# Projections of an attention block computed from high and low parts, and a small gate projection issued on four column strips

## The reference

```
h = modulate(rms_norm(x, norm_mix), shift, scale)          # latent and context tokens
qa, ka, va, qb, kb, vb = split(h @ e_w_in)                 # 512, 128, 128, 512, 512, 512 columns
qa, ka, qb, kb = rms_norm per head of 64; qa, ka get rope on the latent tokens
o_a = window_attention(qa, ka, va, ka_c, va_c, sink)       # 8 query heads, 2 key/value heads
o_b = neighbourhood_attention(qb, kb, vb, kb_c, vb_c, rpb) # 8 heads, a bias table per head
x = x + g1 * (concat(o_a, o_b) @ e_w_out)                  # then a squared-relu MLP
```

```
qkv, z, ba, sc_p, fn_u = split(h @ w_in)                   # ba: 16 columns
beta = sigmoid(ba[:8]);  g = -exp(a_log) * softplus(ba[8:] + dt_bias)
qkv = silu(conv(qkv)) ...                                  # chunked delta rule, gates, merge, SwiGLU
```

## Time and profile before

| | |
|---|---|
| median of 3 runs | 1873.57 us (1872.82 to 1874.22) |
| profiled execution | 1871.45 us, span 1869.6 us |
| busy in the span | PE 1780.8 us (95%), DVE 913.7 (49%), ACT 614.3 (33%), POOL 125.4 (7%) |
| weight loads (PEld) | 1337.9 us (72%) |
| data moved in the first of 40 slices | 388 GB/s, mean of the span 136 GB/s |

### The profile page before, as it was taken

One profiled execution on the slowest core, in us unless ns is written; L12 is line 12 of the kernel. 1 busy time (PEld: TensorE's weight loads), 2 busy tenths in 40 slices (PEclk: granted clock), 3 DMA queues, 4 the chain that ended last, 5 costly groups with the idle time before them and its releaser, 6 DMA issues.

```text
span 1869.6 us, 25422 instructions
## 1 busy us (share of the span) xinstructions
PE 1780.8 (95%) x10086; PEld 1337.9 (72%) x10086; DVE 913.7 (49%) x1704; ACT 614.3 (33%) x1155; POOL 125.4 (7%) x138
## 2 busy tenths in 40 slices
PE   6998899999999999898999999999899899999998
PEld 2443445478888887453679999648579799889997
DVE  2133764263434344345736665344468854445554
ACT  3112554142323232133635444302320044034433
POOL 1001000100000001033000000100115000000000
PEclk9999999999999999998999999899999999999999
DMA  9223774322222223244044443313230334344442
GB/s 388 78 90 146 292 278 186 117 104 95 90 91 90 90 91 144 103 156 162 19 156 157 181 181 137 135 61 125 85 135 1 111 132 165 135 150 168 165 155 85
DMA packets 20886, 253.89 MB, mean 136 GB/s; under 512 B 2208, under 2 KB 4512, under 8 KB 5024
## 3 DMA queue, kind: packets, MB, share of 16 engines
q1 hardware_dynamic: 17712, 242.44, 34.2%
q10 hardware_dynamic: 3056, 9.82, 1.4%
HBM read 251.20 MB, written 1.05 MB: 135 GB/s over the span
## 4 chain that ended last, share of the span: by engine, by line
PE 83%; DVE 8%; ACT 3%; DMA 3%; issue 2%; POOL 1%; DVEq 0%; POOLq 0%; SPq 0%; ACTq 0%
PE bank L498 26%; PE bank L524 13%; PE bank L525 13%; PE bank L526 13%; PE bank L924 4%; PE bank L586 3%; PE bank L661 3%; PE bank L684 2%; PE bank L669 2%; DVE w_lo L1582 1%; DMA weights<-in_ada 1%; ACT w_hi L1187 1%; POOL root L2034 1%; ACT slab L1127 1%; DMA weights<-in_even_in 1%
## 5 line engine op out<-in xcount | busy, mean ns | idle before, releaser
L498 PE MATMUL bank<-slab,weights 128*128 128x256 f32 (+2 forms) x1456 | 445.2, 464 | 3.0 <-DVEq L1691 1.2
L498 PEld LDWEIGHTS bank<-slab,weights 128*128 128x128 f32 (+1 forms) x1456 | 272.8, 189 | 169.7 <-issue 134.2
L1582 DVE TENSOR_TENSOR w_lo<-weights,w_hi 128x1024 fp32r<-128x1024 f32 (+1 forms) x220 | 264.4, 1211 | 93.6 <-ACT w_hi L1187 92.7
L1187 ACT ACTIVATE w_hi<-weights 128x1024 fp32r<-128x1024 f32 (+1 forms) x220 | 228.4, 1046 | 215.9 <-PE bank L526 209.6
L524 PE MATMUL bank<-h_hi,w_hi 128*128 128x256 f32 (+1 forms) x864 | 273.9, 317 | 8.5 <-DVE w_lo L1582 5.9
L525 PE MATMUL bank<-h_lo,w_hi 128*128 128x256 f32 (+1 forms) x864 | 273.4, 316 | 0.0
L526 PE MATMUL bank<-h_hi,w_lo 128*128 128x256 f32 (+1 forms) x864 | 272.0, 315 | 0.0
L524 PEld LDWEIGHTS bank<-h_hi,w_hi 128*128 128x128 f32 x864 | 162.9, 189 | 24.9 <-issue 11.4
L525 PE MATMUL bank<-mlp_hidden_lo,w_hi 128*128 128x512 f32 (+1 forms) x512 | 174.4, 341 | 0.0
L524 PE MATMUL bank<-mlp_hidden_hi,w_hi 128*128 128x512 f32 (+1 forms) x512 | 173.3, 338 | 0.6 <-DVE w_lo L1582 0.6
L526 PE MATMUL bank<-mlp_hidden_hi,w_lo 128*128 128x512 f32 (+1 forms) x512 | 172.7, 337 | 0.0
(11 more groups left out here) (209 smaller groups left out, 2305.2 us busy)
## 6 DMA issues: line engine op xcount, KB each, us to landing
weights<-in_ada SPq DMA_DIRECT2D x36, 2048.0 KB, 7.6
weights<-in_mlp_up SPq DMA_DIRECT2D x16, 2048.0 KB, 8.4
weights<-in_mlp_down SPq DMA_DIRECT2D x16, 2048.0 KB, 8.4
weights<-in_ffn_in SPq DMA_DIRECT2D x11, 2048.0 KB, 7.5
weights<-in_in SPq DMA_DIRECT2D x8, 2048.0 KB, 8.5
weights<-in_gate SPq DMA_DIRECT2D x6, 2048.0 KB, 7.6
weights<-in_ffn_out SPq DMA_DIRECT2D x8, 1408.0 KB, 6.0
weights<-in_even_in SPq DMA_DIRECT2D x4, 2048.0 KB, 13.2
```

The costliest lines, as they stand in the source:

```text
L498: last = mm(b[rows, 0:width], lhsT(k), rhs(k), start=k == 0, stop=k == kc - 1)
L1187: A(split_part(w_hi, q), raw_part(q), ACT.Copy).then_inc(sem("w_hi_ready"), 1)
L1582: V.tensor_tensor(split_part(w_lo, q), raw_part(q), split_part(w_hi, q).bitcast(F32), ALU.subtract)\
```

## The change

- The 14 items of the even projections (a fourteenth for the A heads' values) and the B heads' values use high and low parts. The A keys become item 0, the A queries 1 to 4, the B queries 5 to 8, the B keys 9 to 12. `split_norm` takes the place of the norm's scale and shift.
- The A heads' values are computed feature-major, copied to a buffer and turned by four transposes; the B heads' values use `w_hi` and `w_lo` as the moving operand, all four token groups open at once, over four parts of two chunks.
- Ropes, means and spreads are issued between the items (`even_steps`); the third group's spreads go two by two in side banks.
- The first weight block is loaded in four transfers with semaphores of their own for the first three.
- The `near` table lies where `h_lo` lay, is loaded when the last B value product has closed, and is prepared inside the attention, one head before each even unit from 16 to 30.
- The attentions wait for their values only ahead of the first product with them.
- beta and dt: strips of 32 output partitions as in `ada_block`, issued within key product 0 as the chunks of h come; ScalarE copies the strips; four small matmuls against `fold` add them and put the tokens first.
- `norm_root` is called ahead of `split_norm` instead of inside it.

The diff, cut to its core:

```diff
-SPLIT = {"mlp_up0", "mlp_down0", "mlp_up1", "mlp_down1", "ffn_in", "ffn_out", "gate"}
+SPLIT = {"even_in", "even_in_a", "mlp_up0", "mlp_down0", "mlp_up1", "mlp_down1", "ffn_in", "ffn_out", "gate"}
...
@@ TensorE, split_linear with lead
-                        for q, _ in opened_parts:
-                            pe.wait_ge(sem("w_hi_ready"), q + 1)
-                            pe.wait_ge(sem("w_lo_ready"), q + 1)
                         for k in range(kc - 2):
                             for mi, (q, b) in enumerate(opened_parts):
+                                if k == 0:
+                                    part_ready(q)
                                 triple(b, q, 0, k, mi)
...
@@ TensorE, even projections (the plain products are removed)
+            def even_steps(i):
+                if i == 4:
+                    pe.wait_ge(sem("c0_in"), 16)
+                if i % 4 == 0:
+                    means_of("even", i // 4 - 1)
+                if i in (5, 9):
+                    spread_of("even", i // 4 - 1)
+                if i in (7, 8, 9, 10):
+                    rope("even", i - 7)
+                if i == 11:
+                    rope("even", 4)
...
+            split_linear("even_in", range(3), h_high, h_low, TOK, lambda m: ("even", m),
+                         lambda k, m: pe.wait_ge(sem("mix0_h"), k + 1) if m == 0 else None, lead=True, after=even_steps,
+                         idle=(7, 0))
+            stream.append(["even_in_a", 0, None])
+            for at, t in enumerate((("even", 12), ("va", 0))):
+                q = next_part(at * PART * P, PART * P, t)
+                b = open_group(t)
...
+                if at == 0:
+                    means_of("even", 2)
+            means_of("even", 3)
+            stream.append(["even_in", 3, None])
+            vb = [open_group(("vb", t)) for t in range(4)]
+            for p in range(4):
+                q = next_part(p * PART * P, PART * P, ("vb", 3))
...
+                for t in range(4):
+                    rows = slice(t * P, (t + 1) * P)
+                    for k in range(2):
+                        j = 2 * p + k
+                        mm(vb[t][:, :], h_high(j)[:, rows], wh[:, k, :], start=j == 0, stop=False)
+                        mm(vb[t][:, :], h_high(j)[:, rows], wl[:, k, :], start=False, stop=False)
+                        ins = mm(vb[t][:, :], h_low(j)[:, rows], wh[:, k, :], start=False, stop=j == DC - 1)
...
+                if p == 0:
+                    drained(pe, ("va", 0))
+                    b = open_group(("va", 1), which=0)
+                    for t in range(4):
+                        rows = slice(t * P, (t + 1) * P)
+                        ins = nc.tensor.transpose(b[:, rows], prob[4][:, rows], ident)
+                    close(ins, ("va", 1))
+                if p < 2:
+                    spread_of("even", 2, 2 * p, 2, aside=True)
+                if p == 2:
+                    spread_of("even", 3, aside=True)
             pe.wait_ge(sem("even_roped"), 5)
-            for t in range(4):
-                drained(pe, ("va", t))
-                drained(pe, ("vb", t))
-            attention("even")
+            attention("even", [("va", 1)] + [("vb", t) for t in range(4)])
...
@@ TensorE, second stage
-            w = take_block("in2_ba", 0)
-            for t in range(4):
-                product(("ba", t), DC, lambda k: h[:, k, t * P:(t + 1) * P], lambda k: w[:, k, :], width=16,
-                        before=h_ready("mix2") if t == 0 else None, idle=12 if t == 0 else 0)
-            release_block(("ba", 3))
+            def gates_by_chunk(k):
+                pe.wait_ge(sem("mix2_h"), k + 1)
+                for j in range(k - 3, k + 1) if k % 4 == 3 else ():
+                    strip = slice(j % 4 * STRIP, (j % 4 + 1) * STRIP)
+                    ins = mm(b_ba[strip, :], w_ba[:, j, :], h[:, j, :], start=j < 4, stop=j >= 4)
...
+            def gates_tokens_first():
+                b = open_group(("ba", "tokens"))
+                drained(pe, ("ba", "strips"))
+                for t in range(4):
+                    ins = mm(b[:, t * 16:(t + 1) * 16], ba_row[:, t * P:(t + 1) * P], fold[:, 0:16], start=True, stop=True)
+                close(ins, ("ba", "tokens"))
...
+            for mi in range(4):
+                product(("k", mi), DC, lambda k: w[:, k, mi * P:(mi + 1) * P], lambda k: h[:, k, :],
+                        before=gates_by_chunk if mi == 0 else None, idle=12 if mi == 0 else 0)
+                if mi == 1:
+                    gates_tokens_first()
...
@@ SyncE, the first block of parts
+                if n == parts[0][0]:
+                    for q in range(PARTS):
+                        load(ring[n % RING][:, at:at + PART * P], dram[name][blk][:, at:at + PART * P], f"first_in{q}")
+                        at += PART * P
...
@@ ScalarE
-            norm_shift("mix0", TOK, 0, 0)
+            split_until(PARTS)
+            split_norm("mix0", TOK, 0, 0)
             for i in range(13):
-                if i == 3:
-                    load(near[:, :, :], dram["near"], "near_in")
                 if i == 6:
                     load(consts[:, N_C0:N_C0 + N_C1], dram["c1"], "c1_in")
+                split_until(PART_END[("even", i)] + PARTS)
                 item_raw("even", i)
...
+            for t in (0, 2):
                 copy_out(("vb", t), v0[:, t, 0:512])
+            filled(act, ("vb", 3))
+            load(near[:, :, :], dram["near"], "near_in")
             attention("even")
...
@@ VectorE, attention
+                    if name == "even" and 16 <= i < 32 and i % 2 == 0:
+                        dve.wait_ge(sem("near_in"), 16)
+                        hd = (i - 16) // 2
+                        link(V.scalar_tensor_tensor(out=near[:, hd, :], in0=near[:, hd, :], scalar=HD ** 0.5,
+                                                    in1=k0("near"), op0=ALU.mult, op1=ALU.add))
...
@@ VectorE, split_norm
                 for c in range(DC + 1):
+                    if name == "mix0" and c == 1:
+                        split_until(PARTS)
...
@@ VectorE, even projections
-            norm_scale("mix0", TOK, 0, 0)
+            split_norm("mix0", TOK, 0, 0)
...
+            for i in range(13):
+                split_until(PART_END[("even", i)] + PARTS)
+                if i >= 4 and i % 4 == 0:
+                    group_inverse("even", i // 4 - 1)
+                if i in (8, 9, 10, 11):
+                    rope("even", i - 8)
+                if i in (5, 9):
+                    group_scale("even", i // 4 - 1)
+                if i == 12:
+                    rope("even", 4)
+            split_until(PART_END[("va", 0)] + PARTS)
+            group_inverse("even", 3)
+            split_until(PART_END[("vb", 3)] + 1)
+            group_scale("even", 2)
+            group_scale("even", 3)
+            for t in (1, 3):
+                filled(dve, ("vb", t))
+                V.tensor_copy(v0[:, t, 0:512], bank(("vb", t))[:, :]).then_inc(free(("vb", t)), 1)
```

More of the change, by code:

```diff
@@ L435, in build @@
         ROPE = {
-            "even": ([qk[:, c, 0:LAT] for c in (0, 1, 2, 3, 12)], slice(0, P), k0("rot"), k0("cos"), k0("sin"), rtmp,
-                     [("even", c) for c in (0, 1, 2, 3, 12)]),
+            "even": ([qk[:, c, 0:LAT] for c in range(5)], slice(0, P), k0("rot"), k0("cos"), k0("sin"), rtmp,
+                     [("even", c) for c in range(5)]),
             "uq": ([q1[0:MLA_QK, i, :] for i in range(MLA_HEADS)], slice(0, MLA_QK), k1("rot96")[0:MLA_QK, :],
@@ L512, in linear, with part_ready, next_part, part_used @@
                     release_block(t)
-            def split_linear(name, blocks, hi, lo, width, tag, before=None, lead=False, idle=(0, 0)):
+            def part_ready(q):
+                pe.wait_ge(sem("w_hi_ready"), q + 1)
+                pe.wait_ge(sem("w_lo_ready"), q + 1)
+            def next_part(at, size, tag):
+                q = len(parts)
+                parts.append([len(stream) - 1, at, size, tag])
+                part_ready(q)
+                return q
+            def part_used(ins):
+                used[0] += 1
+                ins.then_inc(sem("part_used"), 1)
+                parts[-1][3] = used[0]
+            def split_linear(name, blocks, hi, lo, width, tag, before=None, lead=False, after=None, idle=(0, 0)):
                 rows, cols, _ = WEIGHTS[name]
@@ L648, in rope, with attention @@
                 close(mm(b[rows, 0:LAT], swap, acts[i], start=True, stop=True), t)
-            def attention(name, idle=0):
+            def attention(name, v_tags, idle=0):
                 a = ATT[name]
@@ L723, in _ @@
             ada_fold(0)
-            items = ITEMS["even"]
-            for blk in range(3):
-                w = take_block("even_in", blk)
-                for mi in range(4):
-                    i = blk * 4 + mi
-                    product(("even", i), DC, lambda k: w[:, k, mi * P:(mi + 1) * P], lambda k: h[:, k, :],
```

(19 more changed lines are left out.)

133 lines of the change are left out of this document (69 added, 64 removed).

## The result

The changed kernel takes 1840.96 us in the median of four runs (1838.70 to 1845.66), beside 1873.89 us (1872.82 to 1877.64) for the kernel before: a ratio of 0.9824, 95% interval 0.9812 to 0.9836. The forecast was 1839.6 us. The profiled execution took 1840.57 us with a span of 1837.7, against 1871.45 and 1869.6: 31.9 us less in the span, where the prediction's sum has 34.0.

What follows compares the result with a forecast made beforehand. TensorE, busy nearly throughout, was taken as the bound. Projections -17.2, attention -0.85 (together -18.0) and beta and dt -16.0 gave -34.0: 1871.45 to 1837.45, plus 2.1 for the median, 1839.6 us; range 1831 to 1853.

Steps and rivals of the forecast that it cites:

- The projections' start: Even projections: first triple near 39.05 us, 3.6 us later than before, behind three subtractions queued on VectorE.
- The clock: Start of the even projections: after TensorE's 3.4 us rest the granted clock falls, costing 1.9 us, between 0 and 2.5.
- Rival 4: Even projections: the lower clock holds through the whole lead, costing 16.8 instead of 1.9 us, total 1854.5 us; chance 0.04.
- lead's toll: Even projections, before the fourth product: TensorE waits 0.95 us because its part is split only after the first product closes.
- the wait for the copy of the A heads' values: Even projections: the next spread needs the bank ScalarE copies those values from, a wait of about 0.9 us.
- item 10's bank: Even projections: 0.5 us lost because this bank is freed only after VectorE scales by the second group's first spread.
- The attention: Even attention: net -0.85 us, with 0.6 us of the moved near operations exposed and gains at the front.
- the front: Start of the even attention: VectorE starts earlier, 0.65 us off, and its 0.81 us wait behind the slow ada block goes.
- Beta and dt: Second stage, before the keys: strips within key product 0 replace four narrow products, 16.0 us off.
- Rival 2: Behind beta and dt: VectorE, not TensorE, sets the time, so only 3.0 us is won, 1852.6 us; chance 0.06.
- the two large terms: Products from parts in the even projections, -17.2 us to the attention's start, and strips for beta and dt, -16.0 us.
- The last step: Whole kernel: from the profiled execution's 1837.45 us to the median of the runs, 2.1 us above it, 1839.6 us.

Runs made afterwards that it cites:

- early: Changed kernel with the first weight parts split as they land, the first ahead of the adaLN copy: 1840.16 us, ratio 0.9810.
- fill: Changed kernel with fifteen instead of seven filling matmuls ahead of the first product: 1839.52 us, ratio 0.9810.
- late_parts: Changed kernel with eleven weight parts split only after the product before them has closed: 1872.41 us, ratio 0.9984.
- after: The changed kernel itself in its first profile, against the kernel before: profiled execution 1840.57 us, median 1840.96 us, ratio 0.9824.
- again: The changed kernel, unaltered, profiled a second time: 1843.22 us, one time.
- again2: The changed kernel, unaltered, run once more: 1839.30 us in the median of four runs, ratio 0.9801.

## Why the prediction was right

**The projections' start** was worked out as 39.05 and came at 39.21; early moved it by the two subtractions that the sum had put there. The clock was taken at 1.9 us between 0 and 2.5: fill gives 2.7 in the profiled execution, just above that range, and 1.3 and 1.5 in two others. The Trainium skill (TensorE: Matmul & The Clock Gate, "The HAM clock gate") has the throttled state as the default that activity releases; by that rule, the trace agrees: a rest of 3.58 us is followed by a clock of 0.50, and with filling in its place it is 1.00. Rival 4 is out with the same windows: from 45 us on the clock is 0.99, though triples still follow chunk by chunk.

**Items and values**: lead's toll 1.0 (0.95 forecast), the wait for the copy of the A heads' values 0.8 (0.9), no wait for item 10's bank (0.5). From first triple to attention at full clock that leaves 117.27 where the sum has 116.45. The remaining 1.3 us (0.8, and the 0.5 for item 10's bank that did not appear) fit a small toll that the sum didn't have: where a triple meets the fp32 matmuls of a spread, on 32 rows, the starts are 0.32 and 0.33 us apart instead of 0.23 (152.03 to 152.35 and 153.40 to 153.73 in the timeline), 0.2 for each of the means and spreads that now stand between triples. That it makes up the difference is argued, no run isolates it.

**The attention** was put at -0.85 and measured at -2.2, but not for the reasons given. At an equal 13.6 or 13.7 us of low clock the six attentions of changed kernels last 194.55 to 195.15 us, the two with the code of before 194.53 and 194.89. So the near operations' 0.2 to 0.5 us are all that the change adds there, and what the front was to gain is one fewer low stretch at a place, which another execution has elsewhere. The term was mis-sized: at equal low clock it is about zero, and the -2.2 are the draw of the profiled execution.

**Beta and dt** gave 15.4 to 15.8 of the 16.0. Two sets of strips cost 2.0 us (1.86), the tokens 0.8 (1.0), and key product 0 with both goes from 1165.56 to about 1174.8, 9.25 us for 8.73: its matmuls take 0.91 us while the chunks arrive, instead of 0.859. The sum took the narrow matmuls' time whole, by its start and end in the trace, so it holds though, by the estimate above, some 5 us of it were the clock. Rival 2 is out: VectorE takes the tokens at 1182.78 (1183.3 forecast) and starts the convolutions at 1189.05 (1189.6), and TensorE never waits for it.

**The end**: of the sum's 34.0 us, 2.1 are missing in the profiled execution. Behind the keys the delta rule takes 2.6 us more; the sum had taken it as unchanged. It is 290.91 us with 10.2 of low clock, 291.7 and 292.1 with 13.6 and 13.7, 293.5 to 294.2 with 17, 295.0 and 295.7 with 20.5 and 297.1 with 23.9, in kernels whose code there is the same. The step that failed is therefore not one of the change but an unstated one: that the one profile of before stands for the stage. Of all twelve it had the least low clock in this stage.

**How much of the hit is luck.** The mechanisms of the two large terms, the triples and the strips, held, and give 30.7 of 33.2 us. That the total came within 2.1 us is partly chance: the projections fell short by 1.9, beta and dt by 0.6 and the delta rule by 2.6, while the even attention and the odd layer gave 1.4 and 1.6 that belong to the clock of that one execution. The last step helped too: the median was put 2.1 us above the profiled execution, as before; after, it lies 0.4 above, which took back 1.7 of the 3.1 us by which that execution's time, 1840.57, had missed 1837.45.

## What to carry to other kernels

A split of a product pays what its triples save (6.87 to 5.6 us) only where the parts are made ahead; price the case in which they aren't (2.55 us a part here, waits and clock together) and look in the trace for the waits of the consumer for the low parts, not at how busy the splitting engines are. Narrow matmuls in front of a long chain cost more than their work: here they ran at the lower clock themselves (0.21 instead of 0.10 us a record), and it stayed low behind them; on column strips, and issued inside a wide product, they cost 1 us per set of four chunks. Before a few microseconds of a stage are called gained or lost, compare the low-clock stretches of both traces: a start that was 4.6 us shorter didn't show in medians of four and five.

## What the runs showed of the hardware that was not expected

The time lost to the lower clock differs between executions of one and the same kernel, which nobody would read from one profile: in the even attention it lasts 6.8, 13.6 and 10.2 us in three profiles of the changed kernel, in the delta rule 17.1, 20.5 and 17.0, and each us of it costs about 0.45 us there (297.1 - 290.9 = 6.2 us for 23.9 - 10.2 = 13.7). It strikes where TensorE has short pauses, in attention and delta rule; the dense stages last nearly the same in all profiles (201.2 to 201.3 us for the second MLP with its norm in eleven and 201.6 in one, 204.63 to 204.67 for the last products). late_parts shows the same on a dense stage: with pauses put between its products, the projections, at 1.00 outside the lead in the changed kernel, had 13.6 us at 0.50. The Trainium skill (TensorE: Matmul & The Clock Gate, "The HAM clock gate") says of a kernel's start that the number of matmuls at the lower clock varies from run to run of the same kernel; the traces agree (after, again and again2 lost 2.7, 1.3 and 1.5 us at their first triples) and show it far inside a kernel as well. Filling the start made no difference to the total, and in fill and early the attention had 13.6 us again; whether a fast start makes a low stretch later likelier, or this is chance, twelve profiles don't say.
